# A second hybrid block's latent mixers: u projected in pairs, all 31 convolution taps on VectorE, tile 1's heads behind the first expert search

## The chip, the cores and the metric

The kernel runs on one core of a Trainium2 chip. The metric is device microseconds of one execution, the median of several. PE is TensorE, DVE is VectorE, ACT is ScalarE, POOL is GpSimd and SP is the engine that only issues transfers. All times are microseconds.

## The reference

Two stacks of two layers run on 256 tokens of width 1024. The first stack (retention, block attention, a short convolution and a gated FFN) hands its output to the second, and only the second stack's two *latent* layers are touched. Each of them computes:

```
q, k, v, u = split(modulate(x) @ w_in)                # q 512, k and v 128 each, u 1024 columns
a, gate = split(u); g = a * sigmoid(gate)             # 512 channels
y = depthwise_conv(g, 31 taps) + conv_b               # along the tokens
o_conv = silu(layer_norm(y) * ln_g + ln_b)
o_attn = softmax(rope(rms(q)) @ [k_ctx, rope(rms(k))]) @ [v_ctx, v]     # 8 heads of 64, 2 key heads, 512 keys
x = x + g1 * (concat(rms(o_attn) * beta_a, rms(o_conv) * beta_c) @ w_o)
# then the expert search and its gather, "peer":
h = modulate(x); q = h @ w_pq                         # 8 heads, two halves each
top 16 of 128 keys per half; top 16 of the 256 sums   # 16 experts per head, 128 per token
x = x + g2 * sum over the 128 experts of gelu(h . u_row) * weight * v_row
```

An expert is one row of u and one of v, 8 KB together.

## The kernel before, in words

The 256 tokens are two tiles of 128 partitions. Every engine has one instruction stream, written out by hand, and nothing but that order and semaphores sets when something runs. The latent layers are written by one loop over `l` in `latent_pe`, `latent_act`, `latent_dve` and `latent_pool`. In each layer:

- **Projections** (`stream_pe_in`, matmuls on L343): q, k and v for both tiles, then u transposed, eight groups of 128 channels (j = 0 to 3 are a, 4 to 7 the gate), eight matmul steps each. ACT copies each out of PSUM (L995). DVE meanwhile normalises and rotates q and k (L1303 to L1341) and raises `rot_ready`. After the last u group PE turns q and k (12 transposes, L337), and DVE makes the padded product g of all four channel groups in one instruction (L1345).
- **Mixer, first part** (`latent_mixer_*`): attention has 16 steps i, eight heads of tile 0 and then eight of tile 1. A step is a score matmul (PE L780), its row maximum (DVE L1436), the exponential (ACT L1109), four transposes (PE L798), their copy (ACT L1117) and the sum over the values (PE L807). In the first twelve steps the convolution runs between them: channel groups 0, 1, 2 on DVE (`tap_step`, L1354 and L1356, three instructions a tap, the three without a wait between them and a wait behind the third), channel group 3 on PE (L790) with diagonal matrices that POOL has made (`stream_pool`, L1223).
- **Mixer, tail** for tile 0: merge of the heads, transposes of the convolved channels (L819), their layer norm, the two halves of the product with w_o (L343), the gates and x, then h, its transposes (L733), queries of head 0 (L343), key scores (L763), and the search for head 0's top keys and pairs on DVE (L1548 to L1655), which writes `IDX`. Steps 13, 14 and 15 of attention lie around this search; their three maxima stand on DVE between its two halves (`within["key"]`).
- **Gather stream**: 256 rows n (tile 0's 128 picks, then tile 1's). POOL issues one indirect transfer a row (L2901, 128 experts, 1.05 MB), into a ring of places that are freed when PE has added a row up. DVE takes the dot product with h (L2846), ACT the gelu and the scale (L2787 to L2794), PE adds the v half up (L2710). The rest of tile 1's mixer and all other searches are put between rows by tables of n (`later`, `SEARCH_AT`). `ring_plan` chooses for each row the place that was used longest ago; a place's first use waits for what `free` names. Of row 0 to 23 nine places take part.

The last rows of the context's own gather are left over to layer 0 of the latent pair (`left_sums`, `left_fetch`): 26 transfers and sums beside its projections.

## Time and profile before

| | |
|---|---|
| time, median of 3 runs | 2952.42 us (2946.86 to 2974.02) |
| span of the profiled execution | 2910.0 us; the runs' median lies 42.4 us above it |
| PE / DVE / ACT / POOL busy | 84% / 72% / 28% / 39% |
| PE's granted clock, mean | 0.915 |
| DMA, mean over the span | 357 GB/s |
| gather stream, layer 0 and layer 1 | first transfer issued at 1419.2 and at 2244.0 |

The profile lists only the span of its execution, not its own time, so the median less the span, 42.4 us, stands for what lies around it. The page's slices of 72.75 us show DMA at about 420 GB/s nearly everywhere, with two gaps: 76 and 191 GB/s at 1310 to 1455 us, and 123 and 50 GB/s at 2110 to 2255 us. These are the two latent mixers.

### The profile page before, as it was taken

What the parts mean: (1) busy time and instruction counts of PE and PEld (TensorE: products, weight loads), DVE (VectorE), ACT (ScalarE), POOL (GpSimd) and SP (SyncE); (2) the same over time, 40 slices, a digit from 0 to 9 for tenths busy, and PEclk for the clock granted to TensorE, in tenths of its full rate; (3) what the DMA queues carried; (4) which work ended last, traced back from release to release, by engine and by line L of the source; (5) the groups of instructions that cost most, each with busy time, mean ns of one, the idle gap of its engine ahead of it and who ended that gap; (6) DMA issues with size and microseconds to landing.
All of it is one profiled execution on the core that took longest, in us unless ns stands there. A gap on an engine that the chain in (4) does not pass through costs nothing.

```text
span 2910.0 us, 27822 instructions
## 1 busy us (share of the span) xinstructions
PE 2441.3 (84%) x8610; PEld 1389.1 (48%) x8610; DVE 2101.8 (72%) x4478; ACT 819.3 (28%) x2274; POOL 1124.6 (39%) x1121
## 2 busy tenths in 40 slices
PE   6996898978898999979798877768797988877876
PEld 3664364756546566656444333324375444332322
DVE  1659479878888978788587777765466977777654
ACT  1231111100012100013443433334324444433443
POOL 1100445766563676461143333334211334333332
PEclk9988897989997899989899899989998999999999
DMA  8348999999999999982499999999831999999997
GB/s 349 144 181 339 369 415 383 374 412 413 416 411 365 402 394 412 395 297 76 191 413 420 420 420 420 420 419 409 351 123 50 414 420 420 420 420 420 420 421 318
DMA packets 183478, 1038.89 MB, mean 357 GB/s; under 512 B 26971, under 2 KB 28978, under 8 KB 99876
## 3 DMA queue, kind: packets, MB, share of 16 engines
q0 software_dynamic: 147456, 805.37, 68.1%
q1 hardware_dynamic: 35292, 230.38, 19.9%
q8 instruction: 70, 1.15, 0.2%
q10 hardware_dynamic: 584, 1.36, 0.1%
q14 instruction: 76, 0.62, 0.1%
HBM read 1032.60 MB, written 4.44 MB: 356 GB/s over the span
## 4 chain that ended last, share of the span: by engine, by line
DMA 33%; PE 31%; DVE 21%; issue 6%; POOL 4%; ACT 3%; SPq 0%; ACTq 0%; DVEq 0%; POOLq 0%
PE PS L343 13%; DMA W<-in_peer_uv,IDX 12%; PE PS L2710 12%; DMA PROJ<-in_peer_uv,IDX 7%; DMA ROWS<-in_peer_uv,IDX 4%; DVE ROWS L1356 4%; DMA ROWS<-in_peer_uv,IDXV 3%; DMA ROWS<-in_peer_uv,COEF 3%; POOL ROWS L2539 2%; DVE ROWS L2331 2%; PE PS L2132 1%; PE PS L2142 1%; DMA ACC<-in_peer_uv,COEF 1%; PE PS L483 1%; DVE PROD L2344 1%
## 5 line engine op out<-in xcount | busy, mean ns | idle before, releaser
L2710 PE MATMUL PS<-W,SCALE 128*128 128x512 f32 x1120 | 539.7, 625 | 99.1 <-ACT SCALE L2794 99.0
L2846 DVE CUSTOM_DVE_ANT_0 W<-W,PS 128x1024 f32<-128x1024 f32 x280 | 337.9, 1219 | 213.5 <-DMA W<-in_peer_uv,IDX 212.9
L2901 POOL DMA_INDIRECT W<-in_peer_uv,IDX x280 | 267.8, 957 | 400.6 <-PE PS L2710 344.9
L2710 PEld LDWEIGHTS PS<-W,SCALE 128*128 128x128 f32 x1120 | 214.2, 199 | 406.0 <-issue 404.9
L2539 POOL DMA_INDIRECT ROWS<-in_peer_uv,IDX x159 | 170.0, 1069 | 366.4 <-DVE IDX L1653 150.5
L2132 PE MATMUL PS<-XT,W 128*128 128x256 f32 x1408 | 307.4, 379 | 0.0
L2132 PEld LDWEIGHTS PS<-XT,W 128*128 128x128 f32 x1408 | 267.8, 190 | 45.5 <-issue 10.1
L2787 ACT ACTIVATE DOT<-DOT 128x1 f32<-128x1 f32 x512 | 103.5, 202 | 602.8 <-DVE DOT L2846 595.9
L343 PE MATMUL PS<-W,XT 128*128 128x512 f32 (+2 forms) x576 | 220.6, 545 | 10.5 <-ACT XT L963 5.7
L343 PE MATMUL PS<-XT,W 128*128 128x128 f32 (+1 forms) x1344 | 218.6, 323 | 3.7 <-ACT XT L1076 3.7
L2794 ACT ACTIVATE SCALE<-C,COEF 128x128 f32<-128x128 f32 x512 | 205.6, 402 | 48.2 <-PE PS L2710 1.4
L343 PEld LDWEIGHTS PS<-XT,W 128*128 128x128 f32 x1344 | 201.0, 194 | 26.8 <-issue 6.7
L2331 DVE CUSTOM_DVE_ANT_0 ROWS<-ROWS,PS 128x1024 f32<-128x1024 f32 x118 | 139.8, 1217 | 42.7 <-DMA ROWS<-in_peer_uv,IDX 40.9
L343 PEld LDWEIGHTS PS<-W,XT 128*128 128x128 f32 x576 | 109.1, 200 | 119.9 <-issue 108.2
L2790 ACT ACTIVATE COEF<-DOT,WGT 128x1 f32<-128x1 f32 x512 | 150.8, 295 | 48.3 <-ACT DOT L2787 0.8
L343 PE MATMUL PS<-W,CT 128*128 128x512 f32 x320 | 150.2, 627 | 6.9 <-ACT CT L1127 4.2
L2901 POOL DMA_INDIRECT ROWS<-in_peer_uv,IDX x44 | 41.6, 946 | 224.2 <-DVE EI L1655 178.9
L2142 PE MATMUL PS<-W,PP 128*128 128x512 f32 x192 | 95.1, 653 | 29.9 <-DVE PP L2499 29.9
L2344 DVE SCALAR_TENSOR_TENSOR PROD<-ROWS,COEF,PROD 128x1024 f32<-128x1024 f32 x80 | 102.7, 1284 | 22.3 <-DMA ROWS<-in_peer_uv,COEF 14.8
L1356 DVE SCALAR_TENSOR_TENSOR ROWS<-ROWS,COLC 128x256 f32<-128x256 f32 x270 | 115.5, 482 | 2.1
L2710 PE MATMUL PS<-ROWS,SCALE 128*128 128x512 f32 x176 | 93.4, 657 | 26.2 <-ACT SCALE L2794 26.0
L2539 POOL DMA_INDIRECT ROWS<-in_peer_uv,COEF x80 | 91.5, 1144 | 43.5 <-DVE PROD L2344 22.4
(422 smaller groups left out, 4066.7 us busy)
## 6 DMA issues: line engine op xcount, KB each, us to landing
W<-in_w_up SPq DMA_DIRECT2D x44, 1024.0 KB, 12.2
W<-in_w_in SPq DMA_DIRECT2D x21, 2048.0 KB, 11.1
W<-in_w_mod SPq DMA_DIRECT2D x7, 4096.0 KB, 12.8
...
```

Source lines behind the costliest of these rows:

```text
L343: ins = nc.tensor.matmul(PS[:, b, cols[0]:cols[1]], lhs(k), rhs(k), start=start and k == 0, stop=stop and k == n_k - 1)
L1356: ins = nc.vector.scalar_tensor_tensor(B["U"][:, j, :], B["PAD"][:, j, k:k + S], tap, B["U"][:, j, :], ALU.mult, ALU.add)
L2132: ins = nc.tensor.matmul(PS[:, 2 * r + half, j * S:(j + 1) * S], up_half(i, half)[:, k, j * P:(j + 1) * P], XT[:, k, :], start=(k == 0), s ...
L2142: ins = nc.tensor.matmul(PS[:, 4 + 2 * t + n, :], HG[r][:, j, t * P:(t + 1) * P], wslot(2 + r, 2, D)[:, j, n * 512:(n + 1) * 512], start=F ...
L2331: nc.vector.tensor_tensor_reduce(beside_slot(l, m), beside_slot(l, m), h, 1.0, 0.0, ALU.mult, ALU.add, DOT[:, 0, m:m + 1]).then_inc(beside ...
L2344: nc.vector.scalar_tensor_tensor(total, slot, coef, total, ALU.mult, ALU.add).then_inc(beside_used, 1)
L2539: nc.gpsimd.indirect_dma_start(beside_slot(l, n), None, one_by_one, bass.IndirectOffsetOnAxis(index[:, n % PICKS:n % PICKS + 1], 0),).then ...
L2710: ins = nc.tensor.matmul(PS[:, SUMS2[t] + h, :], SCALE[:, n % NSCALE, :], v_of(n)[:, h * 512:(h + 1) * 512], start=m == 0, stop=m == PICKS ...
L2790: nc.scalar.activation(COEF[:, t, one], DOT[:, t, one], ACT.Copy, scale=WGT[:, t, one]).then_inc(s.coef_ready, 1)
L2794: nc.scalar.activation(SCALE[:, n % NSCALE, :], ident, ACT.Copy, scale=COEF[:, t, one]).then_inc(s.scale_ready, 1)
L2846: nc.vector.tensor_tensor_reduce(u_of(n), u_of(n), h_of(t), 1.0, 0.0, ALU.mult, ALU.add, DOT[:, t, m:m + 1]).then_inc(s.rows_used, 1)
L2901: nc.gpsimd.indirect_dma_start(pair_slot(n), None, in_pairs, bass.IndirectOffsetOnAxis(IDX[:, t, m:m + 1], 0),).then_inc(pair_signal(fetch ...
```

## The change

- **u in pairs.** In the latent layers the u groups are projected in the order 0, 4, 1, 5, 2, 6, 3, 7, so that a channel group and its gate come together. The twelve transposes of q and k stand behind the sixth group instead of the eighth, and ACT takes q's and k's root after the first group instead of the second. DVE makes g for one channel group at a time (L1379 in the new kernel).
- **Taps.** All four groups' 31 taps are DVE instructions, 124 in all, interleaved over the groups by `TAP_PLAN` so that no tap follows one of its own group; each raises a semaphore and waits for its own group's tap before. 28 taps come before the first maximum, 12 behind each pair of maxima, 48 behind the merge of tile 0. PE's and POOL's part of the convolution is gone.
- **Heads in pairs, tile 1's behind the search.** Tile 0's eight heads run in pairs. All eight of tile 1 come after queries and key scores of head 1 on PE and ACT, and after head 0's search on DVE; two pairs of maxima before row 0's dot product, one after it, one after row 1's. On PE and ACT all eight precede row 0.
- **O's half of tile 0's product** with w_o is computed on PE before the convolved channels are turned.
- **The ring:** the place `MORE` moves ahead to the fifth, and the two places that attention holds (`SLOT_QKT`, `SLOT_PROBS`) become the eighth and ninth.

The diff, cut to its core:

```diff
-(SLOT_ROWS, SLOT_G, SLOT_PROJ, SLOT_KV, SLOT_QKT, SLOT_PROBS, SLOT_W0B, SLOT_W1B, SLOT_W0A, SLOT_W1A,
- SLOT_W2A, SLOT_W2B, SLOT_W3A, SLOT_W3B, SLOT_MORE) = range(15)
+(SLOT_ROWS, SLOT_G, SLOT_PROJ, SLOT_KV, SLOT_MORE, SLOT_W0B, SLOT_W1B, SLOT_QKT, SLOT_PROBS, SLOT_W0A, SLOT_W1A,
+ SLOT_W2A, SLOT_W2B, SLOT_W3A, SLOT_W3B) = range(15)
...
+U_ORDER = (0, 4, 1, 5, 2, 6, 3, 7)
+QK_TURN = 6
+def tap_plan(parts):
+    done, before, plan = [0] * VECTOR_GROUPS, None, []
+    for n, groups in parts:
+        plan.append([])
+        for _ in range(n):
+            free = [g for g in range(groups) if done[g] < TAPS2]
+            g = min(free, key=lambda g: (g == before, done[g], g))
+            plan[-1].append((g, done[g]))
+            done[g], before = done[g] + 1, g
...
+TAP_PLAN = tap_plan([(12, 2), (16, 3), (12, 4), (12, 4), (12, 4), (60, 4)])
...
-            banks.leave_out(5)
-            banks.hold(5, s.conv_ready, 2)
-            for i in range(TAP_HEADS):
-                score(i)
-                taps(taps_at(i))
-                if i >= 2:
+            for i in range(0, QH + 2, 2):
+                if i < QH:
+                    score(i)
+                    score(i + 1)
+                if i:
                     turn_probs(i - 2)
-                if i >= 3:
-                    sum_values(i - 3)
-            head(12)
-            pe.wait_ge(s.conv_ready, 2)
-            banks.put_back(5)
-            for t in range(TT):
-                turn_conv(t)
+                    turn_probs(i - 1)
+                if i:
+                    sum_values(i - 2)
+                    sum_values(i - 1)
             pe.wait_ge(s.merged_ready, 1)
+            banks.banks, banks.i = banks.in_turn() + [6], 0
             turn_branch("O", 0)
             for c in range(2):
                 product("O", 0, c, s.y_read, c + 1)
+            pe.wait_ge(s.conv_ready, 1)
+            for t in range(TT):
+                turn_conv(t)
...
+            score(QH)
+            score(QH + 1)
+            for i in range(QH + 2, TT * QH + 2, 2):
+                if i < TT * QH:
+                    score(i)
+                    score(i + 1)
+                for j in (i - 2, i - 1):
+                    turn_probs(j)
+                for j in (i - 2, i - 1):
+                    sum_values(j)
...
+            def pad(g):
+                dve.wait_ge(s.conv_in_ready, 2 * g + 2)
+                nc.vector.tensor_tensor(B["PAD"][:, g, HALO:HALO + S], B["U"][:, g, :], B["U"][:, 4 + g, :], ALU.mult).then_inc(s.pad_ready, 1)
+
+            def taps(part):
+                for g, k in part:
+                    tap = B["COLC"][:, g, k:k + 1]
+                    if k == 0:
+                        dve.wait_ge(s.pad_ready, g + 1)
+                        ins = nc.vector.tensor_scalar(B["U"][:, g, :], B["PAD"][:, g, 0:S], tap, B["COLC"][:, g, TAPS2:TAPS2 + 1], ALU.mult, ALU.add)
+                    else:
+                        dve.wait_ge(s.dve_step, step_of[g])
+                        ins = nc.vector.scalar_tensor_tensor(B["U"][:, g, :], B["PAD"][:, g, k:k + S], tap, B["U"][:, g, :], ALU.mult, ALU.add)
+                    ins.then_inc(s.dve_step, 1)
+                    step_of[g] = link.count.next()
...
-            for i in range(TAP_HEADS):
-                maximum(i)
-                for k in taps_at(i):
-                    tap_step(k)
-            maximum(12)
+            pad(0)
+            pad(1)
+            taps(TAP_PLAN[0])
+            pad(2)
+            taps(TAP_PLAN[1])
+            pad(3)
+            for i in range(0, QH, 2):
+                maximum(i)
+                maximum(i + 1)
+                taps(TAP_PLAN[2 + i // 2][0:12])
             merge_heads(0)
             link(squares(B["O"][:, 0, :], 4, 0))
+            taps(TAP_PLAN[5][12:])
+            taps_done()
...
-            return {"key": last_maxima}, {
-                2: second_heads, 3: second_stat, 7: second_ratio, 16: lambda: add_product("O", 1, 0, ri[:, 0, 2:3]),
+            return {
+                -2: lambda: second_maxima(QH), -1: lambda: second_maxima(QH + 2), 0: lambda: second_maxima(QH + 4),
+                1: lambda: second_maxima(QH + 6), 2: second_heads, 3: second_stat, 7: second_ratio, 16: lambda: add_product("O", 1, 0, ri[:, 0, 2:3]),
...
                     search(0, 0)
-                    within["key"]()
                     search(0, 1)
+                    later[-2]()
+                    later[-1]()
```

Three places show the new order. The first is DVE from the end of the rotation (`COPY V<-KV`) to the first maxima of tile 0 (NMAX). Before:

```order
L1341 COPY V<-KV 128x256
L1345 TENSOR_TENSOR ROWS<-ROWS 128x4x256
L1436 TENSOR_REDUCE NMAX<-PS 128x1
L1354 TENSOR_SCALAR ROWS<-ROWS,COLC 128x256 x3
L1356 SCALAR_TENSOR_TENSOR ROWS<-ROWS,COLC 128x256 x3
L1436 TENSOR_REDUCE NMAX<-PS 128x1
L1356 SCALAR_TENSOR_TENSOR ROWS<-ROWS,COLC 128x256 x9
```

And of the change:

```order
L1351 COPY V<-KV 128x256
L1379 TENSOR_TENSOR ROWS<-ROWS 128x256 x2
L1386 TENSOR_SCALAR ROWS<-ROWS,COLC 128x256 x2
L1389 SCALAR_TENSOR_TENSOR ROWS<-ROWS,COLC 128x256 x10
L1379 TENSOR_TENSOR ROWS<-ROWS 128x256
L1386 TENSOR_SCALAR ROWS<-ROWS,COLC 128x256
L1389 SCALAR_TENSOR_TENSOR ROWS<-ROWS,COLC 128x256 x15
L1379 TENSOR_TENSOR ROWS<-ROWS 128x256
L1471 TENSOR_REDUCE NMAX<-PS 128x1 x2
```

28 taps now stand before the first maximum, and g is made in four pieces. The second place is PE at the end of tile 0's heads, where L798, L807 and L780 of before (L807, L816 and L798 of the change) are the transposes, value sums and scores. Before, with the convolved channels (L819) first and O's branch (L826) and product (L343) behind:

```order
L780 MATMUL PS<-QKT 128x512
L798 MATMUL PS<-C,ROWS 128x128 x4
L807 MATMUL PS<-V,ROWS 128x64 x4
L819 MATMUL PS<-C,ROWS 128x128 x8
L826 MATMUL PS<-C,ROWS 128x128 x4
L343 MATMUL PS<-W,CT 128x512 x8
L844 MATMUL PS<-C,PROJ_2 128x128 x4
```

And of the change:

```order
L807 MATMUL PS<-C,ROWS 128x128 x8
L816 MATMUL PS<-V,ROWS 128x64 x8
L830 MATMUL PS<-C,ROWS 128x128 x4
L357 MATMUL PS<-W,CT 128x512 x8
L823 MATMUL PS<-C,ROWS 128x128 x8
L848 MATMUL PS<-C,PROJ_2 128x128 x4
```

O's product has gone ahead of the convolved channels (now L823). The third is DVE behind head 0's search, where rows 0 and 1 of the stream are the dot products (ISA, L2889 of the change):

```order
L1698 TENSOR_TENSOR EI<-BV 128x16
L1471 TENSOR_REDUCE NMAX<-PS 128x1 x4
L2889 ISA ROWS,DOT<-ROWS,PS 128x1024
L2889 ISA DOT 128x1
L1471 TENSOR_REDUCE NMAX<-PS 128x1 x2
L1706 TENSOR_REDUCE SUM<-EI 128x1
L1707 RECIPROCAL SUM<-SUM 128x1
L1708 TENSOR_TENSOR WGT<-EI,SUM 128x16
L2889 ISA G,DOT<-G,PS 128x1024
L2889 ISA DOT 128x1
L1471 TENSOR_REDUCE NMAX<-PS 128x1 x2
```

Before, three maxima stood inside the search and none here.

## Rows read from the trace of the kernel before

**Rows 1.** Busy time by stretch: layer 1's mixer, and its stream; DMA share and GB/s last.

```profile
2160.00:2220.00 60.00, 53.80 (x251) 35.52 (x250) 49.12 (x106) 25.02 (x56) 0.00 (x0) 0.97 0.00 1
2520.00:2580.00 60.00, 46.14 (x95) 19.26 (x95) 46.47 (x125) 24.02 (x74) 22.10 (x24) 0.89 1.01 421
```

**Rows 2.** DVE in order of time, layer 1: start, us, line, what; idle before in brackets.

```profile
2124.73 0.28 DVE L1236 RECIPROCAL ri<-rt 128x20 f32<-128x20 f32 x1 [4.04 <-ACT rt L954]
...
2135.12 0.28 DVE L1341 COPY V<-KV 128x256 f32<-128x256 f32 x1
2145.25 1.23 DVE L1345 TENSOR_TENSOR ROWS<-ROWS 128x1024 f32<-128x1024 f32 x1 [9.85 <-ACT ROWS L995]
2148.12 0.69 DVE L1436 TENSOR_REDUCE NMAX<-PS 128x1 f32<-128x512 f32 x1 [1.64 <-PE PS L780]
...
2160.04 3.89 DVE L1356 SCALAR_TENSOR_TENSOR ROWS<-ROWS,COLC 128x256 f32<-128x256 f32 x9
2163.96 0.69 DVE L1436 TENSOR_REDUCE NMAX<-PS 128x1 f32<-128x512 f32 x1
```

**Rows 3.** The page's groups: busy us and mean ns of one after the bar.

```profile
L1356 DVE SCALAR_TENSOR_TENSOR ROWS<-ROWS,COLC 128x256 f32<-128x256 f32 x270 | 115.5, 482 | 2.1
```

**Rows 4.** DVE, layer 0: end of the rotation.

```profile
1313.19 0.29 DVE L1341 COPY V<-KV 128x256 f32<-128x256 f32 x1
```

**Rows 5.** DVE, layer 0: start of the convolution's statistics.

```profile
1371.23 0.70 DVE L1441 BATCH_NORM_STATS2 BN<-PS 128x6 f32<-128x512 f32 x1
```

**Rows 6.** DVE in layer 1's stream: two dot products, each waiting and signalling.

```profile
2271.01 1.22 DVE L2846 CUSTOM_DVE_ANT_0 W<-W,PS 128x1024 f32<-128x1024 f32 x1
...
2272.15 1.22 DVE L2846 CUSTOM_DVE_ANT_0 W<-W,PS 128x1024 f32<-128x1024 f32 x1
```

**Rows 7.** PE in order of time, layer 1: q and k turned; one head's three parts.

```profile
2144.63 1.47 PE L337 MATMUL PS<-C,QR 128*128 128x128 f32 x12
...
2161.30 0.60 PE L798 MATMUL PS<-C,ROWS 128*128 128x128 f32 x4
2161.73 1.00 PE L807 MATMUL PS<-V,ROWS 128*128 128x64 f32 x8
2162.66 1.12 PE L780 MATMUL PS<-QKT 64*128 64x512 f32 x2
```

**Rows 8.** PE, layer 1's tail: channels turned, O's product, head 0's queries.

```profile
2196.40 1.94 PE L819 MATMUL PS<-C,ROWS 128*128 128x128 f32 x8 [1.51 <-DVE ROWS L1356]
...
2200.43 7.13 PE L343 MATMUL PS<-W,CT 128*128 128x512 f32 x16 [1.23 <-ACT CT L1127]
...
2227.23 3.45 PE L343 MATMUL PS<-XT,W 128*128 128x128 f32 x16 [0.68 <-ACT XT L1076]
```

**Rows 9.** PE, layer 0: O's product.

```profile
1373.19 8.94 PE L343 MATMUL PS<-W,CT 128*128 128x512 f32 x16 [1.23 <-ACT CT L1127]
```

**Rows 10.** PE's granted clock (PEclk) in head 0's queries.

```profile
2228.00:2229.00 1.00, 1.00 (x7) 1.00 (x6) 0.00 (x0) 0.00 (x0) 0.00 (x0) 0.50 0.00 0
```

**Rows 11.** DVE, layer 1: merge, statistics, maxima in the search, row 0.

```profile
2196.77 0.19 DVE L1458 RECIPROCAL SUM<-SUM 128x8 f32<-128x8 f32 x1
...
2198.46 0.70 DVE L1441 BATCH_NORM_STATS2 BN<-PS 128x6 f32<-128x512 f32 x1
...
2235.25 1.88 DVE L1436 TENSOR_REDUCE NMAX<-PS 128x1 f32<-128x512 f32 x3
...
2249.86 1.22 DVE L2846 CUSTOM_DVE_ANT_0 ROWS<-ROWS,PS 128x1024 f32<-128x1024 f32 x1 [6.08 <-DMA ROWS<-in_peer_uv,IDX]
```

**Rows 12.** ACT, layer 1: the keys' copy in the tail.

```profile
2208.03 0.59 ACT L1133 COPY QR<-PS 128x512 f32<-128x512 f32 x1 [0.72 <-PE PS L844]
```

**Rows 13.** POOL, layer 1: issues of rows 0, 9 and 15.

```profile
2243.98 1.00 POOL L2901 DMA_INDIRECT ROWS<-in_peer_uv,IDX  x1 [88.24 <-DVE EI L1655]
...
2256.51 0.94 POOL L2901 DMA_INDIRECT ROWS<-in_peer_uv,IDX  x1 [1.58 <-PE PS L2710]
...
2280.31 0.94 POOL L2901 DMA_INDIRECT W<-in_peer_uv,IDX  x1 [4.79 <-PE PS L2710]
```

156 lines of the change are left out of this document (74 added, 82 removed).

## The prediction

> **What bounds the kernel now.** I began with the page's slices of DMA rate. The latent gather streams stand at 420 GB/s with a DMA share of 1.01, and in layer 1's mixer DMA does nothing [rows 1]. So a stream takes as long as its bytes need, and only what delays its first transfer, or lets DMA run dry inside it, moves the end. Next I followed the chain of waits through the mixer to the instruction that frees POOL. It runs: PE's projections of u, DVE's taps, PE's turning of the convolved channels, the norm, the product with w_o, x and h, head 0's queries, keys and search, and row 0's issue [rows 13]. The change is therefore summed as a shift of that issue, twice, and then as what the start of the stream gives back.
>
> **Taps, the price of one.** 9 taps with a maximum before and behind take 3.92 (2160.04 to 2163.96), three groups of three [rows 2]. A group's last tap is waited for: its record of 0.48 [rows 3] plus 0.03 to the next start makes 0.51, so the other two start 0.40 apart. That is an overlap of 0.08 between neighbours. It survives a semaphore raised and one waited for, as long as the wait is already over: dot products that do both start 1.14 apart at 1.22 each [rows 6]. In the new order a tap waits for one at least two back, which by the same 0.40 and 0.48 has ended 0.3 before it could start. I take 0.40; the ends are 0.40 and 0.51.
>
> The Trainium skill (VectorE: DVE Perf Modes, The DRAIN you can't avoid) says instead that the next operation waits for the pipe to empty, and that a semaphore after each of eight copies costs nothing over one after the last. By it the price would be the even mean of the old order, and it would come out as in the second rival.
>
> **Layer 0.** DVE is done rotating at 1313.48 [rows 4]. From there everything is its own work. One product of four groups takes 1.23 [rows 2], and in four pieces I estimate 1.4. 124 taps at 0.40 are 49.6. Eight maxima at 0.61 (0.69 less the overlap) are 4.9. Merge and squares are 1.7 (2196.77 to 2198.46, [rows 11]). New is that DVE then waits for PE: a hand-over and the first half of eight transposes (1.94, [rows 8]), 1.25. The statistics start at 1313.48 + 58.85 = 1372.3 against 1371.2 [rows 5]: 1.1 later. The 28 taps and pieces before the first maximum (12.6) cover PE, which waits for the rotation too, turns q and k in 1.47 [rows 7] and then has two u groups left.
>
> **Layer 1.** DVE now waits 4.04 for ACT's root, and 9.85 for the u groups [rows 2]. The root moves one u group forward and most of the 4.04 goes, but PE is late next: its u groups end at 2144.6, and with the transposes (1.47) before them at 2146.1. The first maximum comes at about 2147.4 instead of 2148.12. From it 4.9 + 96 taps at 0.40 + 1.7 + 1.25 = 46.3 lead to 2193.7 against 2198.46 [rows 11]: 4.8 earlier.
>
> **Tail, both layers.** ACT's copy of the keys waited 0.72 for PE [rows 12], behind O's product; that goes, -0.7 in each layer. In layer 0 O's product took 8.94 against 7.13 [rows 8, 9], part of it at the lower clock, and it was in the way there, so another -1.8. Against it: Y's product followed O's at once and ran at full rate. It now follows about 11 of idle PE (the 48 taps are 19, the product that they cover is over after some 8), eight slow transposes and some 5 of idle again, while DVE norms. Queries after a pause ran at a granted clock of 0.50, which is 1.2 GHz [rows 10], and took 3.45 for 16 records. If all of a 7.13 product ran before the clock rose, 3.6 would be the bound. If the few transposes ahead raise it, nothing. I take 1.3, nearer to the 1.8 of layer 0.
>
> The three maxima inside the search (1.88, [rows 11]) leave the path: -1.9. PE's and ACT's steps for tile 1 leave gaps only. POOL's diagonals go; they waited for nobody.
>
> **Start of the stream.** Eight heads now stand behind the picks. DVE has 6.08 idle before row 0 lands [rows 11] and fits four maxima into it; the other four (2.5) go between rows. Head 1's search thus ends at its old clock time, while DMA starts 1.9 earlier. A pair of rows needs 2.5 at 420 GB/s (1.05 MB). Row 15 was issued 36.3 after row 0 [rows 13]; DMA reaches it 37.5 after its start, itself some 2 later. Of that slack about 1 would be short once the start is 1.9 earlier, and later searches on DVE give back a little more: +1.5 in each layer, bounds 0 and 4.
>
> On PE a head costs 1.12 + 0.60 + 1.00 [rows 7], eight about 20 with overlap. Row 0's place comes free 12.5 after the first issue now [rows 13] and about 20 then. DMA needs the next place about 22.8 after it (nine pairs, less the transfer's own start), so 2.8 to spare. The reordered ring is what makes this hold, since its eighth and ninth places are wanted last.
>
> **Sum.** Layer 0: +1.1 - 0.7 - 1.8 + 1.3 - 1.9 + 1.5 = -0.5. Layer 1: -4.8 - 0.7 + 1.3 - 1.9 + 1.5 = -4.6. Together -5.1: the span goes from 2910.0 to 2904.9, and with the 42.4 that lie around it the time is 2947.3. The runs shown spread over 27, so within 1% (29.5) I call no change.
>
> **Rivals.**
>
> 1. *Taps lose their overlap, slower.* If the wait in front of each tap holds the next one back as the third in a group is held now, a tap costs 0.51. That adds 124 x 0.11 = 13.6 in layer 0 and 96 x 0.11 = 10.6 in layer 1, and gives 2947.3 + 24.2 = 2971.5. It decides from 0.023 more a tap on (5.1 over 220 taps). Against it is the pace of the dot products [rows 6]. Chance 0.08.
> 2. *An even pace.* Waited for or not, a tap costs the mean 3.92 / 9 = 0.436: 220 x 0.036 = +7.9, hence 2955. This is what the Trainium skill's page named above would make of it. The 1.14 between dot products of 1.22 [rows 6] speaks against a pipe that empties each time. Chance 0.13.
> 3. *PE falls to half clock in tile 0's heads, slower.* Its taps kept it busy (53.8 of 60 at a clock of 0.97, [rows 1]). Now a pair of heads is at most 5.4 of PE work in 6.0 of DVE work (two maxima, 12 taps), with a pause in each. If the clock drops in every pause, some 5 of work run at half rate, 2.5 are lost and about 1.4 shows, eight times: +11, 2958. Fully cold it would be up to +30. For it: a pause of 1.5 before 2196.4 was enough to turn channels at half rate [rows 8]. Against it: the records of a head with pauses up to 1.1 ran at full rate. The Trainium skill (TensorE: Matmul & The Clock Gate, A second HAM failure mode: psum-queue depth-cycling) describes such short idles between groups of matmuls as what makes the clock swing. Chance 0.15.
> 4. *The ring is late.* If eight heads take 30 instead of 20, places come 7 after DMA has run dry, in both layers: +14, 2961. It decides from 2.8 more than I count. Chance 0.09.
> 5. *Nothing is given back*: no cold product, no dry DMA, -5.1 - 2.6 - 3.0 = -10.7, hence 2942. Chance 0.12.
> 6. *The gain doesn't arrive*, since searches on DVE after row 15 and not the first issue set the stream's pace for a while; 2952. Against it: the DMA share of 1.01 in the streams. Chance 0.05.
>
> My forecast has 0.38; its own range is 2942 to 2953. The range for 8 in 10 reaches from rival 5, less some spread of the runs, to rivals 3 and 4: 2937 to 2967. Faster by over 1% would need 29.5, more than any sum here gives: 0.02. Slower by over 1% needs rivals 1 and 3 together, or a cold PE throughout: 0.05. Within 1%: 0.93.
>
> **What would show it.** Taps alone between maxima: 12 in 4.9 (0.40 each) or 5.2 or 6.1. Statistics in layer 0 about 1 later after the rotation than now, in layer 1 about 5 earlier. PE's clock in tile 0's heads: 1.00 or dips. Y's product for tile 0: 7.1 or up to 10.7. From the search to row 0's issue 1.9 less. POOL's tenth issue about 20 after its first, and DMA at 420 GB/s between 2.3 and 60 after it; windows below that are what is given back. I am wrong if the mixers got longer, or if the streams after them did.

## The result

The changed kernel took 2968.1 us (median of 20 runs, 2949.7 to 2993.6), the kernel before 2948.9 beside it (2933.0 to 2981.7): a ratio of **1.0066, 95 % interval 1.0044 to 1.0088**, some 19 us slower. The forecast was 2947, range 2937 to 2967. The time is 1 above the range; above all it moved the other way. "Within 1 %" held, with 0.93 on it.

One correction to how the forecast counted: time less span is 1.8 to 1.9 in each listed run of the changed kernel and about 2.2 in those of the kernel before, so the 42.4 "around the span" weren't there. The profile of before is of an execution of some 2912. On later occasions the kernel before had medians from 2910 to 2948, so positions in two profiles can't be subtracted. What can is the length of a stage. Four stages hold the latent part:

- *mixer 0*: from the end of the copy of V behind the rotation to row 0's issue, with a mark at the start of the statistics;
- *stream 0*: from there to the second reading of the sums in layer 0 (DVE, ACC<-PS,ROW, tile 1);
- *mixer 1*: from there to layer 1's first issue, with the same mark;
- *stream 1*: from there to the last reading of the sums.

Below are the means of two profiles of the kernel before (its second is e6_before) and five of the changed one (the first, e2_again, e3_again, e5_changed, e6_changed).

| stage | before | changed | difference (values of the five) | forecast |
|---|---|---|---|---|
| mixer 0, rotation to statistics | 57.4 | 59.4 | +2.0 (58.9 to 60.0) | +1.1 |
| mixer 0, statistics to issue | 46.8 | 47.5 | +0.7 (46.9 to 48.2) | -3.1 |
| stream 0 | 667.5 | 673.5 | +6.0 (671.0 to 677.3) | +1.5 |
| mixer 1, sums to statistics | 110.6 | 109.0 | -1.6 (106.9 to 110.1) | -4.8 |
| mixer 1, statistics to issue | 45.6 | 47.6 | +2.0 (46.8 to 48.2) | -1.3 |
| stream 1 | 657.7 | 664.3 | +6.6 (660.2 to 669.2) | +1.5 |
| together | 1585.6 | 1601.3 | +15.7 | -5.1 |

The two profiles of before differ by 4.7 in their sum (1587.9 and 1583.2), so a term of 1 or 2 isn't to be trusted; the two streams, 12.6 of 15.7, are.

What isn't in these stages lies ahead of them: the span less the rotation's end and the four stages is 8.6 or 8.7 in every profile that is compared here. And there the changed kernel is a little shorter. Its rotation in layer 0 ended at 1309.3 (e5_changed), and at 1305.8 and 1305.5 in two of its variants (e4_order, e5_fill), on occasions on which that of the kernel before ended at 1313.5 and 1312.6 (the first profile, e4_before_gate); in e6_changed it ended at 1336.1, in e6_before at 1341.0. The forecast had no term for this, and its cause wasn't looked for.

### The profile page after: what moved, and what is told of

It is laid out like the page before. It is cut to its first block, busy times and chain, and to the rows that moved or that the text cites. A ratio compares the mean times of both kernels' runs of the same rounds, so it can differ in the third digit from the quotient of the medians.

```text
span 2978.4 us, 27549 instructions
## 1 busy us (share of the span) xinstructions
PE 2446.5 (82%) x8486; PEld 1389.8 (47%) x8486; DVE 2119.5 (71%) x4546; ACT 818.2 (27%) x2272; POOL 1072.2 (36%) x1059
## 4 chain that ended last, share of the span: by engine, by line
PE 34%; DMA 30%; DVE 21%; issue 7%; POOL 4%; ACT 4%; SPq 0%; ACTq 0%; another core or an unknown queue 0%; DVEq 0%; POOLq 0%
PE PS L357 15%; DMA W<-in_peer_uv,IDX 9%; PE PS L2753 9%; DMA QKT<-in_peer_uv,IDX 6%; DMA PROJ<-in_peer_uv,IDX 4%; DMA MORE<-in_peer_uv,IDX 3%; DMA ROWS<-in_peer_uv,IDXV 3%; PE PS L2175 3%; DVE ROWS L2374 2%; DMA ROWS<-in_peer_uv,COEF 2%; DVE ROWS L1389 2%; PE PS L2185 2%; POOL ROWS L2582 2%; DVE PROD L2387 1%; PE PS L816 1%
## 5 line engine op out<-in xcount | busy, mean ns | idle before, releaser
L2753 PE MATMUL PS<-W,SCALE 128*128 128x512 f32 x1120 | 538.1, 623 | 114.0 <-ACT SCALE L2836 113.6
L2889 DVE CUSTOM_DVE_ANT_0 W<-W,PS 128x1024 f32<-128x1024 f32 x280 | 337.9, 1220 | 194.1 <-DMA W<-in_peer_uv,IDX 190.2
L2753 PEld LDWEIGHTS PS<-W,SCALE 128*128 128x128 f32 x1120 | 213.0, 199 | 421.7 <-issue 420.7
L357 PE MATMUL PS<-W,XT 128*128 128x512 f32 (+2 forms) x576 | 235.0, 564 | 39.7 <-issue 32.3
L357 PE MATMUL PS<-XT,W 128*128 128x128 f32 (+1 forms) x1344 | 219.9, 324 | 3.7 <-ACT XT L1084 3.7
L357 PEld LDWEIGHTS PS<-XT,W 128*128 128x128 f32 x1344 | 202.2, 195 | 28.3 <-issue 8.2
L357 PEld LDWEIGHTS PS<-W,XT 128*128 128x128 f32 x576 | 112.0, 205 | 160.7 <-issue 149.2
L2945 POOL DMA_INDIRECT ROWS<-in_peer_uv,IDX x42 | 40.9, 974 | 381.7 <-DVE IDX L1693 182.0
L357 PE MATMUL PS<-W,CT 128*128 128x512 f32 x320 | 158.2, 655 | 14.1 <-ACT H L1164 9.0
L2832 ACT ACTIVATE COEF<-DOT,WGT 128x1 f32<-128x1 f32 x512 | 150.9, 295 | 48.5 <-ACT DOT L2829 1.5
L2387 DVE SCALAR_TENSOR_TENSOR PROD<-ROWS,COEF,PROD 128x1024 f32<-128x1024 f32 x80 | 102.7, 1284 | 19.5 <-DMA ROWS<-in_peer_uv,COEF 10.4
L2753 PE MATMUL PS<-PROJ,SCALE 128*128 128x512 f32 x176 | 92.1, 649 | 28.0 <-ACT SCALE L2836 28.0
L357 PEld LDWEIGHTS PS<-W,CT 128*128 128x128 f32 x320 | 66.6, 212 | 99.7 <-issue 92.4
## 6 DMA issues: line engine op xcount, KB each, us to landing
W<-in_w_mod SPq DMA_DIRECT2D x7, 4096.0 KB, 12.5
W<-in_w_o SPq DMA_DIRECT2D x6, 2048.0 KB, 12.6
```

Of the source, the lines that this page charges most:

```text
L357: ins = nc.tensor.matmul(PS[:, b, cols[0]:cols[1]], lhs(k), rhs(k), start=start and k == 0, stop=stop and k == n_k - 1)
L2387: nc.vector.scalar_tensor_tensor(total, slot, coef, total, ALU.mult, ALU.add).then_inc(beside_used, 1)
L2753: ins = nc.tensor.matmul(PS[:, SUMS2[t] + h, :], SCALE[:, n % NSCALE, :], v_of(n)[:, h * 512:(h + 1) * 512], start=m == 0, stop=m == PICKS ...
L2832: nc.scalar.activation(COEF[:, t, one], DOT[:, t, one], ACT.Copy, scale=WGT[:, t, one]).then_inc(s.coef_ready, 1)
L2889: nc.vector.tensor_tensor_reduce(u_of(n), u_of(n), h_of(t), 1.0, 0.0, ALU.mult, ALU.add, DOT[:, t, m:m + 1]).then_inc(s.rows_used, 1)
L2945: nc.gpsimd.indirect_dma_start(pair_slot(n), None, in_pairs, bass.IndirectOffsetOnAxis(IDX[:, t, m:m + 1], 0),).then_inc(pair_signal(fetch ...
```

## The profile after

VectorE in mixer 0, in order of time (start, us, line, what, count; idle before it in brackets):

```profile
1395.85 4.83 DVE L1389 SCALAR_TENSOR_TENSOR ROWS<-ROWS,COLC 128x256 f32<-128x256 f32 x12
1402.34 0.20 DVE L1493 RECIPROCAL SUM<-SUM 128x8 f32<-128x8 f32 x1 [1.66 <-PE PS L816]
...
1404.03 19.09 DVE L1389 SCALAR_TENSOR_TENSOR ROWS<-ROWS,COLC 128x256 f32<-128x256 f32 x48
1424.39 0.70 DVE L1476 BATCH_NORM_STATS2 BN<-PS 128x6 f32<-128x512 f32 x1 [1.26 <-PE PS L823]
```

48 taps in 19.09, 12 in 4.83: 0.40 each, as the bound from [rows 2, 3] said. But in front of the merge DVE waits 1.66 for the last value sums. TensorE there, same layer, and its steps in the tail (a matmul leaves two records, a transpose one, so x16 are eight matmuls):

```profile
1379.77 2.00 PE L816 MATMUL PS<-V,ROWS 128*128 128x64 f32 x16
...
1398.62 3.68 PE L816 MATMUL PS<-V,ROWS 128*128 128x64 f32 x16
...
1405.67 10.21 PE L357 MATMUL PS<-W,CT 128*128 128x512 f32 x16 [1.23 <-ACT CT L1135]
1423.24 1.97 PE L823 MATMUL PS<-C,ROWS 128*128 128x128 f32 x8 [7.36 <-DVEq L1395]
...
1436.46 10.16 PE L357 MATMUL PS<-W,CT 128*128 128x512 f32 x16 [4.48 <-ACT H L1164]
...
1457.00 3.78 PE L357 MATMUL PS<-XT,W 128*128 128x128 f32 x16 [0.68 <-ACT XT L1084]
```

The same 16 records of value sums take 2.00 and then 3.68: half clock, within tile 0's heads. O's product (L357, 10.21) and Y's (10.16) are longer than 7.13 [rows 8]. The granted clock (PEclk) over the slow value sums and over Y's product:

```profile
1398.62:1402.30 3.68, 3.68 (x17) 3.49 (x16) 2.06 (x6) 0.59 (x1) 0.00 (x0) 0.50 0.00 0
1436.46:1446.62 10.16, 10.16 (x18) 4.34 (x19) 0.75 (x1) 0.43 (x1) 0.00 (x0) 0.70 0.00 0
```

The value sums are wholly at 0.50, Y's product in its first part. And Y's product waits 4.48 for L1164, ScalarE's *reading of O's product*. A bank of PSUM is at fault, as the code suggests and e1_bank shows below: there are seven in turn, and from O's first product bank to Y's the code takes seven. Once O's product has gone first, Y's falls on its two banks, and ScalarE reads those only after the tail's second root, once VectorE has the scale. The diff doesn't show this; the order of `banks.take` does.

POOL at layer 1's first picks, answering [rows 13]: rows 0, 7, 8, 9 and 15:

```profile
2300.55 0.94 POOL L2945 DMA_INDIRECT ROWS<-in_peer_uv,IDX  x1 [182.05 <-DVE IDX L1693]
...
2316.51 0.94 POOL L2945 DMA_INDIRECT QKT<-in_peer_uv,IDX  x1 [7.55 <-PE PS L798]
2325.44 0.94 POOL L2945 DMA_INDIRECT ROWS<-in_peer_uv,IDX  x1 [7.99 <-PE PS L816]
2330.20 0.94 POOL L2945 DMA_INDIRECT ROWS<-in_peer_uv,IDX  x1 [3.82 <-PE PS L2753]
...
2346.00 0.94 POOL L2945 DMA_INDIRECT W<-in_peer_uv,IDX  x1 [2.58 <-PE PS L2753]
```

Row 9, whose place row 0 gives back, comes 29.65 after the first issue (12.5 before, 20 forecast), row 15 45.5 after it (36.3 before). Each wait is for TensorE: scores (L798), value sums (L816), rows' products (L2753). This stream holds a standstill of ScalarE besides (4.73, told with e6_changed); in the eight streams of the changed kernel without one, row 9 came 19.4 to 25.1 after the first issue. The stretches in which DMA runs dry (DMA share and GB/s last, PEclk before them):

```profile
2315.00:2320.00 5.00, 5.00 (x22) 3.65 (x18) 3.63 (x16) 2.45 (x6) 0.94 (x1) 0.50 1.02 431
2320.00:2325.00 5.00, 5.00 (x32) 4.78 (x31) 1.81 (x6) 2.30 (x4) 0.00 (x0) 0.68 0.63 257
2325.00:2330.00 5.00, 3.76 (x7) 1.62 (x7) 4.69 (x11) 4.40 (x14) 0.94 (x1) 0.67 0.60 195
2330.00:2335.00 5.00, 5.00 (x12) 2.15 (x12) 4.62 (x16) 2.97 (x6) 2.82 (x3) 0.99 0.68 229
2335.00:2340.00 5.00, 5.00 (x37) 4.23 (x36) 4.86 (x13) 2.02 (x4) 0.94 (x1) 1.00 0.99 374
```

Three stretches of 5 at 195 to 257 instead of 420. Before, no stretch after the first was under 330 at this point. The second 20 us of layer 1's stream, before and then after:

```profile
2263.98:2283.98 20.00, 15.51 (x65) 8.71 (x64) 15.17 (x53) 9.87 (x25) 4.46 (x5) 0.91 1.01 421
```

```profile
2320.55:2340.55 20.00, 18.76 (x82) 12.52 (x83) 15.95 (x43) 12.13 (x27) 4.70 (x5) 0.85 0.73 265
```

## The experiments

Two theories to begin with. **A:** the loss is made behind the picks; eight heads hold TensorE, ring places come late, DMA runs dry. **B:** it is made in the mixers, by TensorE at half clock, and what stands behind the picks has slack. Stages are given in the order mixer 0, stream 0, mixer 1, stream 1, with row 15's issue after the first (layer 0, layer 1). The changed kernel has 106 to 108, 671 to 677, 155 to 158, 660 to 669 (row 15: 41 to 46, 37 to 45).

### e1_slots: the ring's old order

```
-(SLOT_ROWS, SLOT_G, SLOT_PROJ, SLOT_KV, SLOT_MORE, SLOT_W0B, SLOT_W1B, SLOT_QKT, SLOT_PROBS, SLOT_W0A, SLOT_W1A,
- SLOT_W2A, SLOT_W2B, SLOT_W3A, SLOT_W3B) = range(15)
+(SLOT_ROWS, SLOT_G, SLOT_PROJ, SLOT_KV, SLOT_QKT, SLOT_PROBS, SLOT_W0B, SLOT_W1B, SLOT_W0A, SLOT_W1A,
+ SLOT_W2A, SLOT_W2B, SLOT_W3A, SLOT_W3B, SLOT_MORE) = range(15)
```

> The changed kernel with the ring's old order of places, so that the two places that the heads of tile 1 hold are wanted by rows 4 and 5 instead of 7 and 8. Theory A (the loss is a ring that comes late behind the eight heads, DMA dry at the start of each stream): the issues of rows 4 and 5 wait for the last score and the last value sum, some 16 and 25 us after the first issue in layer 1 and 14 and 21 in layer 0, DMA is short of about three more pairs at 2.5 each, and each stream, from its first issue to the second reading of the sums (669.2 and 672.2 in the changed kernel, 657.4 and 667.8 in the one before), gets 5 to 8 longer; the time goes up by 10 to 16. Theory B (the loss is PE's half clock in the mixers and what comes after the picks has slack): the streams stay within 2 us of 669.2 and 672.2, and the time stays within its noise.

Ratio to before 1.001 (0.9988 to 1.0033). Stages 106.5, 672.8, 156.1, 664.2; row 4's issue came at 12.9 and row 5's at 18.8 in layer 0, where DMA at 2.5 a pair wants them at 10.0 and 12.5 after the first, and yet the streams are as long as in e2_again (672.0, 664.3). Theory A's number (5 to 8 longer) is wrong. Row 15 was issued at 40.9 in both layers, as in e2_again: TensorE gets to row 6's product no sooner in either order. DMA ran dry at rows 4 and 5 instead of 8 and later, for about the same in all (see behind e4_order). So a late place seems to cost once; the latest of the first sixteen counts.

### e1_ahead8 and e1_ahead4: heads of tile 1 into the stretch of 48 taps

```
 # TensorE
             product("O", 0, c, s.y_read, c + 1)
+        for i in range(QH, QH + AHEAD, 2):    # scores, then the pair's transposes and value sums
+            score(i)
+            score(i + 1)
         pe.wait_ge(s.conv_ready, 1)
# VectorE
         link(squares(B["O"][:, 0, :], 4, 0))
+        for i in range(QH, QH + AHEAD, 2):
+            maximum(i)
+            maximum(i + 1)
+            taps(the next 12 of the 48)
```

The edit is cut here; it also leaves O's two banks out of the turn until Y's product has gone.

> The changed kernel with all eight heads of tile 1 moved from behind the picks into the stretch of 48 taps, a pair of maxima ahead of each 12 taps; the O product's two banks are left out meanwhile, so that the Y product for tile 0 no longer waits for their reading. What is left of the change is the taps on VectorE and u in pairs. Theory A (late ring): both streams fall back to the lengths of the kernel before (657.4 and 667.8) or 1 to 2 above, since POOL finds its places free; from rotation to the first issue it is 4.9 longer for eight maxima (0.61 each) and 2.6 shorter for the bank; together about 12 faster than the changed kernel, 7 slower than the kernel before. Theory B (half clock): PE has 20 us of heads in the 24 us of taps, so its clock stays up, the Y product takes 7.1 to 8.5 and not 10.2, but the streams keep their 669 and 672; 3 to 4 faster than the changed kernel at most.

> The changed kernel with four of tile 1's eight heads in the stretch of 48 taps and four left behind the picks, and the Y product's banks as in the run with eight. Theory A (late ring): the last score and value sum come about 4 and 10 us after the first issue, ahead of when rows 7 and 8 are wanted (17 to 20), so both streams are at 657 to 659 and 667 to 669; rotation to first issue 2.5 longer for four maxima and 2.6 shorter for the bank, so no change there; about 14 faster than the changed kernel, that is 0 to 5 slower than the kernel before. Theory B (half clock): as with eight, streams unchanged, 2 to 3 faster than the changed kernel.

Ratios 1.007 (1.0047 to 1.0093) and 1.0059 (1.0037 to 1.008). Streams: 667.3 and 658.1 with eight ahead, 668.5 and 658.2 with four. **Both streams are back where they were before the change**: A is right about where that loss is made. But rotation to statistics grew from 59.4 to 78.5 and 73.5, by 19 and 14 instead of 5 and 2.5. VectorE in e1_ahead8, at the first maximum of tile 1:

```profile
1391.29 1.29 DVE L1474 TENSOR_REDUCE NMAX<-PS 128x1 f32<-128x512 f32 x2 [11.62 <-PE PS L799]
```

I had put the scores behind O's product on TensorE, so the 48 taps stood still for 11.62 behind a maximum. That edit made the same error as the forecast: it counted an operation's own time, not what is queued in front of the one that it waits for.

### e1_bank: Y's product on other banks

```
             turn_keys(1)
+            banks.i += 2
             for c in range(2):
                 product("Y", 0, c, s.mix_read, c + 1)
```

> The changed kernel with one difference: the Y product for tile 0 takes the two banks of the convolved channels' transposes and not those of the O product. Its wait for ScalarE's reading of the O product (4.48 in layer 0) shrinks by 2.6, to ScalarE's scaling of the turned channels; rotation to first issue 2.6 shorter in layer 0 and 1 to 2.6 in layer 1, streams unchanged, 4 to 5 us in all. If the wait was not for the bank but for something that comes late with it, nothing moves.

Ratio 1.0007 (0.9977 to 1.0037). TensorE, layer 0:

```profile
1407.99 8.89 PE L357 MATMUL PS<-W,CT 128*128 128x512 f32 x16 [1.71 <-ACT CT L1136]
```

The wait is 1.71, for ScalarE's scaling of the turned channels. Statistics to issue: 44.1 and 45.7, against means of 47.5 and 47.6: 3.4 and 1.9 shorter. The wait was for the bank. Stream 0 came to 677.5; see e6_changed.

### e2_spread: heads laid into gaps

```
 PE:  tile 0's last pair    + score(8), score(9)          DVE: before merge_heads(0)       + maximum(8), (9)
      behind O's product    + turn and sum 8, 9                before add_product("Y", 0)  + maximum(10), (11)
      behind turn_keys(0)   + score(10), score(11)
      behind turn_branch("Y", 1)  + turn and sum 10, 11
      behind the picks: heads 12 to 15 alone              Y's product: banks of keys 0 and Y's turning
```

> The changed kernel with tile 1's heads laid into gaps: heads 8 and 9 are scored beside tile 0's last pair and their maxima stand where VectorE waits for the merge; their transposes and value sums follow the O product; heads 10 and 11 are scored in the pause ahead of Y's turning, their maxima stand where VectorE waits for the Y product, their sums where TensorE waits for h; only heads 12 to 15 stay behind the picks. The Y product doesn't take the O product's banks. Theory A (late ring): the places for rows 7 to 9 come free in time, streams from first issue to the second reading of the sums 668 to 669 and 658 to 659 (as with four heads ahead), rotation to first issue in layer 0 as with the banks alone (103.4) or 1 above, first sums of layer 0 to first issue of layer 1 154.7 or 1 above; against the changed kernel -22, against the kernel before -3 to -5. Theory B (work behind the picks is harmless, the loss lies in the mixers' half clock): streams stay at 672 and 669, and only the bank's part is gained, -7 against the changed kernel.

Ratio 0.9988 (0.996 to 1.0016). Stages 104.8, 668.4, 155.4, 659.1; row 15 at 38.0 and 36.5. The expected -22 is -14 against the mean of the changed kernel's profiles; A's streams came as stated. It undoes the loss and wins nothing over the kernel before. What is left of the change, taps and u in pairs, is worth about nothing with the heads laid out like this: mixer 0 104.8 (102.6 and 105.7 before), mixer 1 155.4 (155.4 and 157.1).

### e2_warmheads and e2_warmtail: TensorE kept busy

```
+ nc.tensor.matmul(PS[:, 7, 0:512], ident, C[:, 0:512], start=True, stop=True)    (n times; nobody reads it)
  warmheads: 1 behind each pair of tile 0's scores
  warmtail:  7 behind O's product, 2 behind keys 0, 2 behind keys 1, 4 behind turn_branch("Y", 1)
```

> The changed kernel with one matmul of 512 columns, whose result nobody reads, behind each pair of scores of tile 0's heads on TensorE. If the half clock there (value sums 3.68 for 16 records, against 2.00) is what pauses bring about, the granted clock stays at 1.00 in tile 0's heads, VectorE's wait at the merge (1.66 in layer 0, 1.61 in layer 1) is gone, and rotation to first issue is 1.5 shorter in each layer. If the clock falls all the same, the added matmul is a cost of 0.9 to 1.8 a pair and the wait at the merge grows to 3 to 7. Theory A sees no other change: streams as in the changed kernel, 4 to 12 longer than before.

> The changed kernel with matmuls of 512 columns, whose result nobody reads, in TensorE's pauses: 7 behind the O product, 2 ahead of Y's turning, 2 ahead of the Y product, 4 ahead of h's turning. If the pauses are what costs the clock, the turned channels take 1.1 instead of 1.97, the Y product 7.1 instead of 10.2, h's turning 1.1 instead of 1.97 and head 0's queries 1.95 instead of 3.78: stats to first issue 4 to 6 shorter in each layer, 8 to 12 in all. If the clock is granted by something else, the added work (0.9 each, or 1.8 at half clock) only stands in the way: 0 to 6 longer in each layer.

Ratios 1.003 (1.0005 to 1.0055) and 1.0029 (1.0008 to 1.005). In warmheads, layer 0, three of tile 0's four groups of value sums ran at full rate, as this one; the last took 3.13:

```profile
1368.93 2.00 PE L820 MATMUL PS<-V,ROWS 128*128 128x64 f32 x16
```

Rotation to statistics was 58.4 against 59.4, so B's part in tile 0's heads is about 1 in a layer. Warmtail was undecided. In layer 1 the turned channels took 1.10, but the bank still made this pause, and the product behind it began at half clock (granted 0.71 in its mean):

```profile
2241.94 10.01 PE L357 MATMUL PS<-W,CT 128*128 128x512 f32 x16 [3.63 <-ACT H L1172]
```

Statistics to issue: 46.2 and 48.5, no gain in layer 1. Streams stayed at 672.2 and 663.6, 674.1 and 664.0.

### e4_order: places against search

```
-  0: maxima 12, 13   1: maxima 14, 15   2: second_heads   3: second_stat
+  2: maxima 12, 13   3: maxima 14, 15   5: second_heads   6: second_stat
```

After e1_slots there was a second reading of A: head 1's search on VectorE stands behind maxima that wait for TensorE. This order moves the two delays apart.

> The changed kernel with VectorE's maxima of heads 12 and 13 behind row 2 and of 14 and 15 behind row 3, instead of behind rows 0 and 1, the merge and the squares behind rows 5 and 6; head 1's first search step stays behind row 1 and thus comes ahead of four maxima and of the waits for TensorE in front of them. Theory A1 (what lengthens the streams is that places come free late): scores, value sums and with them row 0's product come later by 3 to 6 (row 9's issue at 27 to 29 after the first instead of 23 to 25), and both streams get 3 to 6 longer than 672 and 664. Theory A2 (what lengthens them is head 1's search, which stands on VectorE behind maxima that wait for TensorE: its first picks came 32.1 after the first issue in layer 1, against 25.7 before the change): the search is done 2 to 4 earlier, and the streams get 1 to 3 shorter although the places come later.

Ratio 1.0058 (1.0042 to 1.0074), on an occasion where the kernel before took 2910. VectorE in layer 1, the end of head 1's search in e4_order, its first issue having been at 2247.87:

```profile
2274.22 0.23 DVE L1693 TENSOR_SCALAR IDX<-EI,BASE 128x16 int32<-128x16 f32 x1
```

and in e2_again, first issue at 2283.41:

```profile
2314.60 0.23 DVE L1693 TENSOR_SCALAR IDX<-EI,BASE 128x16 int32<-128x16 f32 x1
```

The search ends 26.4 after the first issue instead of 31.2, nearly as early as before (25.7). Yet POOL in e4_order:

```profile
2247.87 0.94 POOL L2945 DMA_INDIRECT ROWS<-in_peer_uv,IDX  x1 [184.24 <-DVE IDX L1693]
...
2276.90 0.94 POOL L2945 DMA_INDIRECT ROWS<-in_peer_uv,IDX  x1 [9.67 <-PE PS L816]
...
2294.57 0.94 POOL L2945 DMA_INDIRECT W<-in_peer_uv,IDX  x1 [1.62 <-PE PS L2753]
```

Row 8 at 29.0, row 15 at 46.7, and streams of 677.7 and 669.1: 5.7 and 4.8 longer than e2_again's. A1 stands, A2 falls. Over all kernels a stream's length follows row 15's issue: in layer 1 36.3 gives 657.4 and 658.0, 37.0 gives 660.2, 40.9 gives 663.6 to 664.3 (seven profiles), 45.4 and 46.7 give 669.2 and 669.1. It follows what DMA lacks, too. Counted over the first 80 us of layer 1's stream against 421 GB/s, DMA lost 3.9 us in the kernel before, 6.0 in e5_changed, 9.4 in e1_slots, 10.7 in e2_again and 14.1 in the first profile of the changed kernel; the streams are 657.4, 660.2, 664.2, 664.3 and 669.2.

### e3_root, e3_gate, e3_both, e5_fill: what is left to win

```
 e3_root:  e2_spread, and   -  if i == (2 if beside else 1):   +  if i == 2:   ahead of ScalarE's root
 e3_gate:  e2_spread and, ahead of turn_h(0):   pe.wait_ge(s.merged_ready, 2);  3 unread matmuls of 512 columns
 e3_both:  e3_gate and 1 unread matmul behind each pair of tile 0's scores
 e5_fill:  e3_gate and 4 ahead of turn_conv, 2 ahead of turn_branch("Y", 0), 1 ahead of Y's product
```

> The kernel with spread heads, but ScalarE takes the root of the queries' and keys' norms behind the second u group again, as before the change, and not behind the first. In layer 1 VectorE's wait for it is 4.04 again and not 0.58, its rotation ends 3.4 later, and the stats start 3.4 later if VectorE is what sets them; in layer 0, where rotation does not wait for it, nothing. +3.4 against the spread kernel. If the u groups (TensorE) set the end of that stretch instead, +0 to +1.

Ratio 1.0017 (0.9987 to 1.0048). The wait for the root was 5.46 instead of 0.58, as forecast or more; sums to statistics 112.4 against 110.2 in e2_spread, and also 110.2 in e3_gate, whose projections were as slow as these (16.06 and 16.04). The root moved is worth about 2 in layer 1.

> The kernel with spread heads, and three matmuls of 512 columns, whose result nobody reads, ahead of h's turning; TensorE starts them when x for tile 0 is summed, some 4.3 before h is ready. At full rate they take 2.7, at half clock 5.4. If they keep or bring the clock up: h's turning 1.1 to 1.3 instead of 1.97 and head 0's queries 1.95 instead of 3.79, the search 2.5 earlier in each layer, -5 against the spread kernel, -8 against the kernel before. If the clock stays at half: they end 1 after h is ready, +1 in each layer, +2 in all.

> The kernel with spread heads, with the three matmuls ahead of h's turning and one matmul of 512 columns behind each pair of scores of tile 0's heads. As the run before, and in tile 0's heads the clock stays up as it did in the changed kernel with these matmuls alone. In the spread kernel VectorE doesn't wait at the merge any more (two maxima stand there), so the second part has nothing left to win: within 1 of the run before. If a later TensorE step profits from it (O product, first transposes), up to -3 more.

Ratios 0.9982 (0.995 to 1.0014) and 0.9957 (0.9917 to 0.9997). TensorE in layer 0, first e2_spread (head 0's queries, Y's product for tile 1), then e3_gate with the unread matmuls ahead:

```profile
1441.35 3.79 PE L357 MATMUL PS<-XT,W 128*128 128x128 f32 x16 [0.68 <-ACT XT L1100]
...
1446.22 9.38 PE L357 MATMUL PS<-W,CT 128*128 128x512 f32 x16
```

```profile
1425.25 2.79 PE L902 MATMUL PS<-C 128*128 128x512 f32 x6
...
1430.83 2.05 PE L357 MATMUL PS<-XT,W 128*128 128x128 f32 x16 [0.73 <-ACT XT L1104]
...
1433.66 7.13 PE L357 MATMUL PS<-W,CT 128*128 128x512 f32 x16
```

Statistics to issue 42.1 in both layers, after 45.4 and 45.2. The second part of e3_both changed nothing in the stages (42.4 and 42.1).

> The kernel before the change, with nothing but the three unread matmuls ahead of h's turning, started when x for tile 0 is summed. There h's turning took 1.97 and head 0's queries 3.45 at a granted clock of 0.50. If they come to 1.1 and 2.0 as in the spread kernel: statistics to first issue 2.3 shorter in each layer, 4 to 5 in all, 0.15 %. Then what the spread kernel with these matmuls gains over the kernel before is theirs, and the spread of the heads is worth nothing by itself. If its clock was high enough before them (value sums stand right there), +-0.

Ratio 0.9994 (0.9982 to 1.0006). On the kernel before the same three matmuls, with h's turning at 1.09, left head 0's queries in layer 1 at 3.28 (3.45 before): statistics to issue 46.7 and 44.7. The granted clock was 1.00 in the three matmuls and 0.59 in layer 1's queries behind them, where e3_gate's queries in layer 0 had 1.00. So the gain isn't theirs alone. Transposes and value sums of two heads stand just ahead in both kernels and don't explain the difference; what does wasn't found.

> The spread kernel with the three unread matmuls ahead of h's turning, and further unread matmuls of 512 columns in the pauses before: four behind heads 8 and 9's value sums (ahead of the turning of the convolved channels), two ahead of Y's turning, one ahead of the Y product. If pauses are what halves the clock, the turned channels take 1.1 instead of 1.97, the Y product 7.1 to 8 instead of 9.7 to 10, h's turning and the queries stay at 1.1 and 2.05: statistics to first issue 2 to 3.5 shorter in each layer than with the three alone, -4 to -7 in all; about 12 below the kernel before. If the clock falls during the 8.8 of the O product or the taps all the same, the added work runs at half rate, ends after the convolved channels are ready and costs up to 3 in each layer.

Ratio **0.9939 (0.9923 to 0.9956)**, 2891.7 against 2910.1: faster than both kernels. Stages 100.0, 667.4, 149.5, 658.3. TensorE in layer 0, convolved channels turned and Y's product:

```profile
1363.83 1.09 PE L830 MATMUL PS<-C,ROWS 128*128 128x128 f32 x8 [2.05 <-DVEq L1431]
...
1373.83 7.13 PE L357 MATMUL PS<-W,CT 128*128 128x512 f32 x16
```

Y's product is at 7.13 in both layers: the half clock in front of it did come from pauses, and they can be filled. Not every step gained: head 0's queries took 2.05 in layer 1 but 3.50 in layer 0. It is 10.4 below before's mean in the four stages, out of 18 in the time; the other 8 lie ahead of them (the rotation ended at 1305.5, in the first profile of before at 1313.5).

### e2_again, e3_again, e5_changed, e6_changed, e6_before: how steady is all this

> The changed kernel itself once more, for a second profile. In its first one ScalarE stood still for 4.73 some 5 us after layer 1's first issue, with its input ready, and not in layer 0; with the banks alone the same stood in layer 0 (4.88) and not in layer 1. If this belongs to the place in the code, the second profile shows it in layer 1 again, streams 672 and 669. If it is a matter of the moment, it may be in the other layer, in both or in neither, and the streams are 672 without it and 5 longer with it in layer 0, 664 and 669 in layer 1.

> The changed kernel a third time, for one more profile: how often ScalarE stands still for 4 to 5 within 10 us of a layer's first issue. So far in one of four streams of this kernel. Streams of 672 and 664 without it, 5 more with it.

> The changed kernel on the same chip as the last version, timed in as many rounds, so that the two are compared there: streams of 672 and 664 (5 more where ScalarE stands still behind the picks), 0.4 to 0.7 % above the kernel before. If this difference belongs to single chips, it comes out near nought or above 1 % here.

> The changed kernel on the same chip. Where TensorE runs at half clock ahead of the picks, its first scores stand later behind the first issue, the places for rows 7 to 9 come later (14, 20 and 23 instead of 10 to 12, 17 to 19 and 19 to 22) and the streams are 672 and 664 instead of 671 and 660. On a chip where the kernel before takes 2940 or more: 0.4 to 1.2 % above it; where that takes 2910: 0 to 0.3 %.

> The kernel before the change, for a second profile of it, on the same chip as the changed kernel's next one. So far its stages are known from one profile, of an execution of 2912 in all, while the same program took 2943 to 2948 on two other chips. If those chips are slow in the stages ahead of the latent mixers alone, the four stretches (rotation to first issue 106.7, stream 667.8, sums to first issue 157.1, stream 657.4) come out within 1 each on any chip, and the 14 to 18 by which profiles of the changed kernel exceed them are the change's. If a slow chip slows the mixers of this kernel too, by TensorE at half clock, the mixers come out 3 to 6 longer there, the streams as they were, and part of the 14 to 18 is the chip's.

Ratios of the changed kernel: 1.004 (1.0014 to 1.0066), 1.0122 (1.0056 to 1.0188, two runs), 1.0005 (0.9994 to 1.0016), 1.005 (1.0032 to 1.0068). On one occasion of five it cost nothing, though its four stages were 8.2 above before's mean (1593.8); half of that is made up ahead of them, where its rotation ended 4.2 sooner than before's. There its streams were 671.0 and 660.2, and in layer 1 its scores began 1.6 ahead of the first issue, since the product before them had run faster; row 7 came at 10.2 instead of 14.1. The second profile of before gave 102.6, 667.2, 155.4 and 658.0, its mixers 1.7 to 3 shorter than in the first, its streams the same; on that occasion (before 2939) the changed kernel lost 0.5 % and 19.3 in the four stages, of which 4.9 came back ahead of them. O's product in layer 0 in e6_before:

```profile
1399.93 7.13 PE L343 MATMUL PS<-W,CT 128*128 128x512 f32 x16 [1.23 <-ACT CT L1127]
```

7.13, where [rows 9] had 8.94 and e4_before_gate 8.96: the 1.8 that the forecast meant to win there is not in every execution.

ScalarE stood still in two of the changed kernel's ten streams (stream 1 of the first profile, 4.73; stream 0 of e6_changed, 4.87) and once in e1_bank (4.88). With four heads behind the picks instead of eight it did so in nine streams more: once in e1_ahead4 (4.27) and in both of e2_spread, e3_root, e3_gate and e3_both (4.1 to 6.5). In e6_changed:

```profile
1452.26 1.07 ACT L1125 COPY ROWS<-PS 128x512 f32<-128x512 f32 x2 [4.87 <-remote]
```

Each time it began 4.5 to 7.2 after the first issue. With eight heads behind the picks that stream was some 5 longer (669.2; 677.3; 677.5). With four it wasn't (667.7 to 668.5 and 658.6 to 659.7, against 667.4 and 658.3 in e5_fill, which shows none); row 15 came at 35.2 to 38.0 all the same. No profile of the kernel before shows it. Since the same code has it in one execution and not in another, the place in the code isn't enough; what holds ScalarE wasn't found.

## Why the prediction was wrong

**Taps** held: 0.396 each. Rivals 1 (0.51) and 2 (0.436) are out. Records of 0.48 start 0.40 apart even with a semaphore between them. The section of the Trainium skill that the forecast named (VectorE: DVE Perf Modes, The DRAIN you can't avoid) has the next operation wait for the pipe to empty, but adds that one which isn't held starts earlier; the forecast passed over that, and the trace agrees with it.

**Mixer 0 up to the statistics** was nearly right, +2.0 for +1.1; what lacked was the wait at the merge (1.66 in the first profile), rival 3 in small. It was given +11 if it came; e2_warmheads prices it at about 1 in a layer. The Trainium skill (TensorE: Matmul & The Clock Gate, A second HAM failure mode: psum-queue depth-cycling) has short idles between groups of matmuls make the clock swing, and the trace agrees (value sums 2.00, then 3.68); but the price of the swing depends on DVE's slack there, which the page can't know.

**Tail.** The step that failed: "It now follows about 11 of idle PE ... I take 1.3". Three things were in it. The product was at half clock for longer: it took 8.5 to 10.2 instead of 7.13, which is 1.4 to 3.1 and not 1.3. It waited besides for its bank (e1_bank: 3.4 and 1.9), a wait to which the forecast gave nothing. And of the -1.8 from O's product there is nothing to win where it takes 7.13 before the change too, as in e6_before. Forecast for statistics to issue -3.1 and -1.3, measured +0.7 and +2.0.

**Layer 1's head start.** The wait for the root did shrink from 4.04 to 0.58; e3_root gives it 2. But sums to statistics gained 1.6 and not 4.8. Most of the rest lies on TensorE in front of it. From the sums to the projections it took 16.7 instead of 15.4 in the mean, and the projections 15.3 instead of 13.9, as told below.

**Start of the stream** is the main failure, twice +1.5 forecast, +6.0 and +6.6 measured. "DMA needs the next place about 22.8 after it ..., so 2.8 to spare" asked about the tenth place alone and about an undisturbed TensorE. That the eight heads take about 20 was right: 17.9 to 20.8 from the first score to the last value sum, 26.2 and 26.4 with a standstill. Without one row 9 came at 19.4 to 25.1, close to the 22.8. But the places behind follow from the same queue: rows 0 to 6 are multiplied only after eight heads. Row 15, issued at 36.3 to 37.2 before, was wanted at some 38 by the forecast's own count (15 pairs of 2.5 and what it added for row 9); it came at 40.9 to 46.0 in nine of ten streams, and the forecast never asked when TensorE would get to it. "Head 1's search thus ends at its old clock time" was wrong too (31.2 after the first issue for 25.7), but e4_order shows that this cost nothing. Rival 4 had the right mechanism, a ring that is late, and a chance of 0.09. Its condition, heads that take 30, wasn't met, since the threshold had been derived from one place only; and its size was too large, +14 on top of the 3.0 in the sum against 12.6 measured for both. With the 7.1 that the tails missed it would give 2968.4, as measured, but by luck: the 4.4 too many stand for the 4.1 that both mixers lost ahead of their statistics.

Of the account of +15.7, shown by experiment are the streams (e1_ahead4, e1_ahead8, e4_order), the bank (e1_bank) and, for Y's product, the clock in the tail (e5_fill). How the rest divides is within the spread of single profiles.
